# A token tile's two expert rows: the second gather adds in place instead of VectorE summing two buffers

## The reference

```python
x = layer_norm(ALPHA * x + m, ln1_g, ln1_b)
x = layer_norm(ALPHA * x + hier_moe(x, ...), ln2_g, ln2_b)

def hier_moe(x, ...):
    # top-1 group of 4, then top-2 experts of the 4 in that group
    h = silu(einsum('nd,edf->nef', xt, moe_w1)) * einsum('nd,edf->nef', xt, moe_w3)
    h = h * gates[..., None]          # zero but for a token's two experts
    y = einsum('nef,efd->nd', h, moe_w2)
```

## Time and profile before

| | us |
|---|---|
| median of three runs | 1202.25 |
| lowest, highest run | 1200.2, 1205.96 |
| the profiled execution | 1202.03 |
| its span, first to last instruction | 1200.3 |
| TensorE busy in the span | 1121.1 |
| VectorE busy in the span | 808.0 |
| ScalarE, GpSimd busy in the span | 537.6, 194.2 |

### The profile page before, as it was taken

The page is one execution under the profiler, slowest core; times in us unless marked ns, Lnnn a source line. Parts: engine busy times, 40 slices in busy tenths (PEclk is TensorE's granted clock), DMA queues, the critical chain, the costliest instruction groups (busy, mean ns, idle before and its releaser), DMA issues.

```text
span 1200.3 us, 20513 instructions
## 1 busy us (share of the span) xinstructions
PE 1121.1 (93%) x5736; PEld 995.4 (83%) x5737; DVE 808.0 (67%) x1532; ACT 537.6 (45%) x703; POOL 194.2 (16%) x189
## 2 busy tenths in 40 slices
PE   6999999999999999999999988899998999999970
PEld 6999999999999999978888867687887887777760
DVE  4666544374446456767777758797755898888884
ACT  4465343363336346422223312655544666656530
POOL 1000000010001000102222223406101132322322
PEclk9999999999999999999999999899999999999995
DMA  5331599747973742544444225896866789888563
GB/s 182 132 107 50 143 147 121 94 114 115 118 91 122 282 170 85 173 140 156 148 168 141 106 93 190 294 330 220 288 232 236 276 320 354 294 297 292 197 225 140
DMA packets 87274, 221.58 MB, mean 185 GB/s; under 512 B 19152, under 2 KB 45808, under 8 KB 80944
## 3 DMA queue, kind: packets, MB, share of 16 engines
q1 hardware_dynamic: 57824, 129.90, 33.1%
q0 software_dynamic: 18160, 59.53, 14.8%
q10 hardware_dynamic: 11232, 31.47, 13.7%
HBM read 133.75 MB, written 87.11 MB: 184 GB/s over the span
## 4 chain that ended last, share of the span: by engine, by line
PE 53%; DMA 16%; DVE 13%; issue 7%; ACT 6%; ACTq 2%; DVEq 2%; SPq 0%; POOL 0%; POOLq 0%
DMA y_scr<-yb 11%; PE ps_h L1484 9%; PE ps_vb_c L903 8%; PE ps_va_b L292 7%; PE ps_vb_c L292 7%; PE ps_va_b L903 6%; PE ps_o L1462 6%; PE ps_g L292 3%; PE ps_x L1451 2%; DMA gate<-g_scr 2%; DVE w_lo L1117 1%; PE ps_r_i L916 1%; ACT x_hi L1112 1%; PE ps_h L1513 1%; DVE yb L562 1%
## 5 line engine op out<-in xcount | busy, mean ns | idle before, releaser
L1484 PE MATMUL ps_h<-x_hi,xt_hi 128*128 x312 | 125.5, 402 | 3.0 <-issue 2.4
L292 PE MATMUL ps_vb_c<-x_hi,w_hi 128*128 (+1 forms) x320 | 114.6, 358 | 9.7 <-DVE x_lo L467 9.6
L1484 PE MATMUL ps_h<-x_hi,xt_lo 128*128 x312 | 122.0, 391 | 0.0
L1484 PE MATMUL ps_h<-w_lo,xt_hi 128*128 x312 | 121.7, 390 | 0.0
L292 PE MATMUL ps_vb_c<-x_hi,w_lo 128*128 (+1 forms) x320 | 113.9, 356 | 0.0
L292 PE MATMUL ps_vb_c<-x_lo,w_hi 128*128 (+1 forms) x320 | 113.3, 354 | 0.0
L292 PE MATMUL ps_va_b<-x_hi,w_lo 128*128 (+1 forms) x320 | 112.7, 352 | 0.0
L292 PE MATMUL ps_va_b<-x_hi,w_hi 128*128 (+1 forms) x320 | 112.6, 352 | 0.0
L292 PE MATMUL ps_va_b<-x_lo,w_hi 128*128 (+1 forms) x320 | 111.8, 349 | 0.0
L482 DVE SCALAR_TENSOR_TENSOR xc<-vb,par,xc 128x416 f32<-128x416 f32 (+1 forms) x60 | 39.1, 652 | 53.3 <-ACT xc L353 49.5
L1117 DVE TENSOR_TENSOR w_lo<-x_hi_p,x_hi 128x2048 f32 (+1 forms) x30 | 68.5, 2289 | 8.5 <-ACT x_hi L1112 6.8
(11 more groups left out here) (361 smaller groups left out, 2713.4 us busy)
## 6 DMA issues: line engine op xcount, KB each, us to landing
x_hi_p<-in_w SPq DMA_DIRECT2D x48, 1024.0 KB, 7.1
o_scr<-x_raw ACTq DMA_DIRECT2D x42, 512.0 KB, 7.7
w_lo_p<-xs_scr SPq DMA_DIRECT2D x41, 512.0 KB, 5.8
o_scr<-w_lo_p SPq DMA_DIRECT2D x41, 512.0 KB, 6.1
w_raw<-in_w_in POOLq DMA_DIRECT2D x19, 512.0 KB, 3.7
xs_scr<-x_raw ACTq DMA_DIRECT2D x18, 512.0 KB, 10.5
x_raw<-in_x_t SPq DMA_DIRECT2D x20, 416.0 KB, 3.4
x_hi_p<-y_scr SPq DMA_DIRECT2D x16, 512.0 KB, 4.2
```

What stands on the lines that cost most here:

```text
L292: mm = pe.matmul(ps[i][:, 0:CHUNK], w[:, i, k], x[:, k, bass.ds(c * CHUNK, CHUNK)], start=(k == 0 and n == 0), stop=(k == KT - 1 and n == 2))
L1484: mm = pe.matmul(ps_h[par][:], x[:, par, k], w[:, bass.ds(at, 1), k].rearrange("p o n -> p (o n)"), start=(k == 0 and n == 0), stop=(k == ...
```

## The change

The second gather of a tile no longer has a buffer of its own. GpSimd issues the first gather into `v[b]`, waits on `s_v[b]` until that has landed, and issues the second into the same buffer with an add (`compute_op=ALU.add`), so that the transfer itself adds onto what is there. VectorE's sum (L1718) goes, and its statistics become the first to read the tile, after both gathers. The buffers `v1`, the semaphore `s_sum` and GpSimd's waits on it go too; they had kept a second buffer from being filled again too early. In a step that has both, `put` of one tile now stands ahead of `fetch` of another in GpSimd's list.

```diff
--- before.py
+++ after.py
@@ -1173,7 +1173,6 @@
 
         raw = [ew.w13_raw[:].rearrange("p k n -> p (k n)")[:, i * D:(i + 1) * D] for i in range(4)]
         v = [rows(wreg[i], 4, 5)[:, 0] for i in (2, 3)] + [consts[:, P:P + D]] + raw[0:2]
-        v1 = [x_raw[:].rearrange("p a b c -> p (a b c)")[:, 0:D], sb("v1", [P, D])[:]] + raw[2:4]
 
         part = lambda i, n, e: v[i][:, n * NT * NE:(n + 1) * NT * NE].rearrange("p (a b) -> p a b", b=e)
         tot2, inc2, later, big = part(0, 0, NT), part(0, 1, NT), part(1, 0, NT), part(1, 1, NE)
@@ -1208,8 +1207,8 @@
             sem(n) for n in ("s_later", "s_cnt2", "s_need", "s_row", "s_pairs"))
         s_rec, s_put, s_fin, s_idf, s_eps = (sem(n) for n in ("s_rec", "s_put", "s_finin", "s_idf", "s_eps"))
         s_v = [sem(f"s_v{i}") for i in range(5)]
-        s_sum, s_bn, s_mv, s_std, s_rstd, s_fx, s_fn, s_y = (
-            sem(n) for n in ("s_fsum", "s_bn2", "s_mv2", "s_std2", "s_rstd2", "s_fx", "s_fn", "s_yout"))
+        s_bn, s_mv, s_std, s_rstd, s_fx, s_fn, s_y = (
+            sem(n) for n in ("s_bn2", "s_mv2", "s_std2", "s_rstd2", "s_fx", "s_fn", "s_yout"))
         first, second = bass.ds(0, 1), bass.ds(1, 1)
         LAST = len(GROUPED) - 1
 
@@ -1383,9 +1382,7 @@
                 if b >= 3:
                     pool.wait_ge(s_13lo, 2 * NE)
                 elif not early(f, 2):
-                    taken, landed = count(pool, f - 1), count(pool, f * 16 - (32 if fixed else 16))
-                    pool.wait_ge(s_sum, 1)
-                    pool.wait_ge(s_sum, taken)
+                    landed = count(pool, f * 16 - (32 if fixed else 16))
                     if not (b == 2 and used == 0):
                         pool.wait_ge(s_y, 16)
                         pool.wait_ge(s_y, landed)
@@ -1399,9 +1396,13 @@
                 if not fixed:
                     pool.wait_ge(s_idf, 1)
                     pool.wait_ge(s_idf, copied)
-                for i, to in enumerate((v[b], v1[c])):
-                    at = fin[:, f, 1 + i:2 + i] if fixed else id_f[:, b, 1 + i:2 + i]
-                    pool.indirect_dma_start(to, None, o_scr[0:STEPS * P], bass.IndirectOffsetOnAxis(at, 0)).then_inc(s_v[b], 16)
+                at = [fin[:, f, i:i + 1] if fixed else id_f[:, b, i:i + 1] for i in (1, 2)]
+                pool.indirect_dma_start(v[b], None, o_scr[0:STEPS * P], bass.IndirectOffsetOnAxis(at[0], 0)).then_inc(s_v[b], 16)
+                there = count(pool, used * 32 + 16)
+                pool.wait_ge(s_v[b], 16)
+                pool.wait_ge(s_v[b], there)
+                pool.indirect_dma_start(v[b], None, o_scr[0:STEPS * P], bass.IndirectOffsetOnAxis(at[1], 0),
+                                        compute_op=ALU.add).then_inc(s_v[b], 16)
 
             def put(tile):
                 f, b, _, _ = tile
@@ -1420,10 +1421,10 @@
                     get, add, norm = tiles
                     stored = (h, h - 1) if par == 0 else (h, h)
 
+                    if norm:
+                        put(norm)
                     if get:
                         fetch(get, stored)
-                    if norm:
-                        put(norm)
                 if isinstance(s, int) and 5 <= s < 7:
 
                     if s == 5:
@@ -1715,8 +1716,6 @@
                 f, b, c, used = tile
                 n, m = TAIL if early(f, 1) else P, c % 2
                 dve.wait_ge(s_v[b], used * 32 + 32)
-                dve.tensor_tensor(v[b][0:n], v[b][0:n], v1[c][0:n], ALU.add).then_inc(s_sum, 1)
-                dve.wait_ge(s_sum, f + 1)
                 for i in range(2):
                     ins = dve.bn_stats(stats[0:n, i], v[b][0:n, i * 512:i * 512 + 512])
                 ins.then_inc(s_bn, 1)
```

## The result

The changed kernel takes 1237.1 us (median), the kernel before 1201.4 in the runs beside it: a ratio of 1.029, 95% interval 1.0244 to 1.0335. It is slower by some 35 us (35.7 by the medians), where +7.6 was forecast; the time lies above the range. The profiled execution took 1236.85 us with a span of 1235.1, 34.8 longer than before.

What follows compares the result with a forecast made beforehand. From about 920 us, TensorE's waits for VectorE's `hid` (5.4 us) were taken to come first, then VectorE's waits for second gathers. Terms: -2.9 + 4.5 + 2 + 4 = +7.6 us, giving 1209.6 us; range 1199 to 1221.

Steps and rivals of the forecast that it cites:

- rival B: Every tile: the add is dear, +4.6 us per tile, gathers become the bound; +24.9, 1227 us; chance 0.15.
- term 3: Tiles 7 to 13, last steps: scatter ahead of the gather and late adding gathers cost +2 us (-0.6 to +5).
- B's own sign: What would show the dear add: adding gathers above 10 us everywhere.
- What bounds the kernel now: From about 920 us: TensorE's 12 waits for VectorE's `hid`, 5.4 us, come first; then sums waiting for second gathers, 2.9.
- Term 1: Steps of tiles 0 to 2 and 6 to 9: removing VectorE's sums ends TensorE's waits, -2.9 us (-1.5 if half stays).
- term 4: The end, tiles 15 and 16: two gathers in series after the last store cost +4 us (+1.6 to +6.2).
- Gap and price of the add: Second gather: issued 0.3 us after the first lands; the add costs one more read, +1.5 us (0 to +4.6).
- Term 2: Tiles 3 to 5: late second gathers, 3.6 us at tile 3 and 7.6 at tile 5, cost +4.5 (-1.9 to +11).
- A (hidden): Tiles 3 to 5: the second gather stays hidden, landing within 5.4 us, so not slower; 1199.5 us; chance 0.2.
- The estimate of 3.2 us by the Trainium skill: One gather: 2.0 us plus bytes over 436 GB/s; by it the second gather would stay hidden.
- the rule of two source reads: Adding gather: a reducing DMA is slow through two source reads per chunk, at half a copy's bandwidth; hence +1.5 us.
- C: Only the end moves: TensorE's waits have other causes, the middle is neutral, the end pays 2 to 4; 1205; chance 0.15.

Runs made afterwards that it cites:

- The kernel with the held gather: Changed kernel with a plain, overwriting second gather, held on GpSimd by two small copies after the first landed: 1231.2 us, ratio 1.0217.
- one pair of runs: Four first buffers, first gather one tile ahead: with the adding gather 1210.6 us, with plain gathers and VectorE's sum 1204.8 us.
- by 2.6 in the other: First gather two tiles ahead in the last steps: with the adding gather 1205.7 us, with plain gathers and VectorE's sum 1203.1 us.
- the kernel with most buffers: Adding kernel with first gathers two tiles ahead in the last steps, plus new buffers for the last four tiles: 1200.5 us, ratio 0.9989.

## Why the prediction was wrong, step by step

**Which case it was.** None of those written down. The forecast had the sign and the mechanism (VectorE's statistics wait for a late second gather, TensorE for `hid`), rival B had a dear add, but as load on the DMA engines (1227). What happened is more than B's size, by the forecast's mechanism; B's own sign, adding gathers above 10 us everywhere, was not there (6.4 to 10.5, median 7.7). The step that failed is the size of the lateness, in term 3 above all: +2 us were forecast for tiles 7 to 13, and +17.3 came in from tile 6 to tile 13, since each step's lateness was counted by itself and with the best landing, where it goes on into the next step and the landings are longer.

**What bounds the kernel now**: right. The path from gather to `hid` to TensorE is where the time came in.

**Term 1, the sum's removal (-2.9)**: too small and not to be had. Taken out by itself it gave 5.8 us. TensorE's waits for `hid` fell by 2.0 only (5.4 to 3.4), its other listed waits by 1.9, and from tile 15's first gather to the end it was 1.6 shorter (31.0 to 29.4), where the last two sums were; those the prediction had in term 4. In the changed kernel the term rested on "the gathers of these tiles land well ahead" for tiles 0 to 2 and 6 to 9. The statistics of tiles 1, 2, 7 and 8 waited 3.4, 3.7, 2.6 and 6.4 us, and by tile 2, where 0.9 us were to be won, they stood 4.8 us later. TensorE's waits in 1055:1140, where 2.0 was to vanish:

```profile
PE ps_ht L1500 <- DVE hid L1643: 7.7, 4, 3.3
```

**Gap and price of the add.** GpSimd's gap was forecast at 0.3 us; from landing to the next issue it was 0.77 (996.46 to 997.23 in the chain), and the adding issue took 1.57 against 0.94 for the plain second gather. Of engine time, the add was forecast at 1.5 us. GpSimd's queue in 920:1225, for the kernel with the plain second gather and for the changed one:

```profile
q0 software_dynamic: 7248, 26.35, 25.2%
...
q0 software_dynamic: 7104, 25.82, 32.5%
```

76.9 us of 16 engines against 99.1, for a little less data: 23.8 more at equal MB, 1.4 per tile. So that estimate held. It was the wrong quantity: per tile the landing grew by 2.4 us (5.3 to 7.7), and the landing is what stands in the chain.

**Term 2, tiles 3 to 5 (+4.5)**: the lateness of one tile was right, the discount wrong. Tile 3 was forecast 3.6 us late, and its statistics moved 3.6 beyond those of tile 2 (8.4 against 4.8); tile 5 was forecast 7.6 late and moved 9.5 beyond tile 2. The prediction cut the 6.3 us that would arrive to 4.5, since "the queues drain in between". They did, and nothing came sooner. Two stretches in which TensorE stood still and the two after each (last columns: granted clock, DMA share, GB/s):

```profile
984.00:986.00 2.00, 0.00 (x0) 0.00 (x0) 2.00 (x3) 1.99 (x3) 1.45 (x1) 1.00 0.08 31
986.00:988.00 2.00, 1.96 (x11) 1.97 (x11) 2.00 (x1) 1.00 (x2) 1.55 (x1) 0.56 0.54 119
988.00:990.00 2.00, 2.00 (x8) 1.63 (x7) 2.00 (x4) 1.68 (x2) 1.04 (x1) 0.59 0.97 393
...
1008.00:1010.00 2.00, 0.00 (x0) 0.00 (x0) 2.00 (x2) 1.99 (x3) 1.66 (x1) 1.00 0.00 0
1010.00:1012.00 2.00, 1.70 (x8) 1.71 (x9) 2.00 (x2) 1.30 (x2) 0.70 (x1) 0.53 0.48 102
1012.00:1014.00 2.00, 2.00 (x9) 1.72 (x8) 2.00 (x4) 1.27 (x2) 0.00 (x0) 0.61 0.94 373
```

The engines are almost idle (0.08 and 0.00) while TensorE stands. As soon as it runs, they are full again (0.97, 0.94), so the next pair of gathers meets the same load: 10.01 and 8.42 us at tile 3, 9.90 and 9.65 at tile 5. The mean load did not tell how long a single transfer in the chain would take.

**Term 3, tiles 7 to 13 (+2)**: the largest miss. From tile 6 to tile 13 the shift grew from 12.6 to 29.9, +17.3. Three things failed. The best landing, 4.3, was taken where the typical one was needed: from the adding gather's issue to the statistics, tiles 10 to 14 took 7.0 to 8.8 us, against a forecast of 6.1 with the gap. The wait of the scatter behind a GpSimd that stands at the first gather was left out: tile 7's norm ended at 1105.6, its scatter went out at 1109.58, behind tile 8's adding gather. And each step's lateness was treated as its own, 1.2 us for the worst and 0.8 for all others together. But the next store comes from the step that was late, so the lateness of each step adds to that of the last: from tile 9 to tile 13 it went from +17.8 to +29.9.

**Term 4, the end (+4)**: right in kind, half its size. From the first gather of tile 15 to the statistics of tile 16 it was 14.35 us before and is 22.50, +8.2; forecast 3.3 to 4.8, at most 6.2. The statistics of tile 15 came 12.85 us after that gather (8.48 before): +4.4 against 1.9. The first gather of tile 16 came 9.66 us after that of tile 15; 7.2 were forecast. Again each landing was taken near its best. Two slips beside it change little: the store ahead of tile 15's first gather is the last but one, and the low bound, 1185.4 against 1183.63, is +1.8 and not +1.6.

**Rivals.** A (hidden) is refuted from tile 1 on, whose statistics waited 3.4 us. Even before the change four sums waited, not the three that the prediction read (2.9 us more, at tile 15). The estimate of 3.2 us by the Trainium skill (DMA: Bandwidth & Descriptors, "Anatomy of one DMA — SWDGE (gpsimd) path"), beside which it stood, agrees here only with the best plain gathers: these took 4.2 us, 0.94 of it the issue, but 5.2 to 6.4 at the median, and an adding one of the changed kernel 6.4 at best. Of the other page (Collectives: The Full Stack, "The bandwidth ceiling: the fold count and why AG ≠ RS ≠ AR") the rule of two source reads agrees with the queue: 0.52 MB plain take 1.5 us of all engines, with the add 2.9. C is refuted by TensorE's waits.

**TensorE's own busy time** was in no term. Its rows from 920 us on, before and after (columns as above):

```profile
920.00:1200.00 280.00, 235.95 (x1127) 191.20 (x1125) 221.75 (x269) 147.46 (x177) 75.21 (x61) 0.95 0.75 268
...
920.00:1235.00 315.00, 245.18 (x1128) 199.54 (x1126) 202.74 (x252) 147.89 (x177) 80.51 (x61) 0.90 0.74 238
```

The same work took 9.2 us longer there (7.9 over the whole span). The last store goes out 29.1 us later (1197.0, before 1167.9); TensorE's listed waits grew by 20.0 (`hid` 21.2 more, the others 1.2 less), so they and the 9.2 account for it. Behind both stalls the rows of term 2 show a granted clock of 0.53 to 0.61 in two stretches of 2 us each, where the kernel before had 1.00 throughout these stretches: near the lower of the clock's two levels, 1.2 GHz. The kernel with the held gather shows the same without an add: 245.5 us busy from 920 us on, against 236.6 in the one with the plain second gather. A stall here cost its own length and some of the work after it.

**What stays open.** Whether the add is worth more or less than VectorE's sum once it is off the chain: the sum was ahead by 5.8 us in one pair of runs and by 2.6 in the other, at the edge of what the intervals tell, but in both pairs the kernel with the sum was also rid of GpSimd's wait for the first gather, and the kernel with most buffers was not tried with a sum. And the part of the loss that the lower clock makes was not tested by itself: the 9.2 us are its size only if nothing else made TensorE's work longer.

## What to carry to other kernels

Folding an add into the second transfer replaces two transfers in parallel by two in series: cost that as a whole landing (measured in the loaded stretch, at its median, not its best), not as engine time, and ask first what the second has to follow. In a loop of steps that feed one another, lateness per step adds up (here 2.5 us of chain in each of 17 tiles became 24.7 us); count it for every step, and discount nothing for queues that drain unless a row shows it. If an accumulating transfer is wanted, send the plain part earlier: a tile ahead gave back 26.5 of the 35 us, two tiles ahead with more buffers all of them, and even then the kernel was no faster than with the sum that the add had replaced.

## What the hardware did that was not expected

- An accumulating gather of 128 rows of 4 KB occupied GpSimd for 1.57 us at its issue against 0.94 of a plain one, and landed after 7.7 us against 5.3 (medians; the changed kernel and the one with the plain second gather).
- Scatters that wait for one another left at 4.1 us intervals at the very end (1189.20, 1193.32, 1197.40, in the kernel with the first gather one tile ahead), with no other transfer under way.
- Two small copies on GpSimd, 0.18 us each, with a wait behind each, held a gather for 1.35 us, and 17 such holds cost a kernel of 1212 us some 19, of which some 9, by the profiles, are TensorE's longer busy time.
